# First attention: weighing the values as three bfloat16 products, with the turned rows split by ScalarE and VectorE

## What is computed

```python
def block(args):
    ...
    logits = jnp.einsum('bqhd,bqkd->bqhk', qb.astype(f32), k_sel.astype(f32)) * attn_scale
    logits = jnp.where(valid[:, :, None, :], logits, -jnp.inf)
    p = jax.nn.softmax(logits, axis=-1)
    o = jnp.einsum('bqhk,bqkd->bqhd', p, v_sel.astype(f32))
    return o.astype(qb.dtype)
```

## Time and profile before

| | |
|---|---|
| Time, median of 3 runs | 1764.91 us (1761.79 to 1765.24) |
| The profiled execution: its time | 1763.56 us |
| The profiled execution: its span | 1761.8 us |
| TensorE busy | 1724.0 us (98%) |
| VectorE busy | 1182.8 us (67%) |
| ScalarE busy | 813.6 us (46%) |
| GpSimd busy | 887.1 us (50%) |

### The profile page before, as it was taken

The page is one execution under the profiler, slowest core; times in us unless marked ns, Lnnn a source line. Parts: engine busy times, 40 slices in busy tenths (PEclk is TensorE's granted clock), DMA queues, the critical chain, the costliest instruction groups (busy, mean ns, idle before and its releaser), DMA issues.

```text
span 1761.8 us, 30529 instructions
## 1 busy us (share of the span) xinstructions
PE 1724.0 (98%) x11938; PEld 891.6 (51%) x11938; DVE 1182.8 (67%) x2237; ACT 813.6 (46%) x1628; POOL 887.1 (50%) x805
## 2 busy tenths in 40 slices
PE   8999999999999999999999999999999999999998
PEld 5534455555444466544544455544455555555543
DVE  5759889999999788532345677966155565654637
ACT  4523554443322577412332468733255555555710
POOL 0511443652671222696911177969556555772750
PEclk9999999999999999999999999999999999999999
DMA  9010111102321112212512346512211111111512
GB/s 396 32 54 36 55 49 62 71 37 102 161 96 48 73 67 103 120 48 96 201 63 94 111 145 198 186 54 96 68 40 53 56 42 51 35 52 55 216 58 96
DMA packets 53375, 161.87 MB, mean 92 GB/s; under 512 B 7056, under 2 KB 21776, under 8 KB 49008
## 3 DMA queue, kind: packets, MB, share of 16 engines
q1 hardware_dynamic: 49008, 136.36, 21.8%
q0 software_dynamic: 4224, 23.56, 3.4%
HBM read 129.35 MB, written 27.39 MB: 89 GB/s over the span
## 4 chain that ended last, share of the span: by engine, by line
PE 67%; DVE 20%; ACT 4%; POOL 3%; DMA 3%; issue 2%; SPq 0%; DVEq 0%; ACTq 0%; POOLq 0%
PE ps L1422 28%; PE ps L1901 15%; DVE small L2684 6%; PE ps L1416 4%; DVE arena L2437 4%; PE ps L1762 2%; PE ps L1445 2%; PE ps L1486 2%; PE ps L1544 2%; PE ps L1920 2%; DMA hT<-in_mods 2%; PE ps L1518 1%; PE ps L1694 1%; PE ps L1459 1%; PE ps L1526 1%
## 5 line engine op out<-in xcount | busy, mean ns | idle before, releaser
L1422 PE MATMUL ps<-hT,W 128*128 128x512 bf16 x2424 | 536.5, 380 | 4.1 <-ACT arena L2004 3.2
L1422 PEld LDWEIGHTS ps<-hT,W 128*128 128x128 bf16 x2424 | 235.7, 98 | 288.3 <-issue 10.2
L989 POOL TENSOR_TENSOR W<-W 128x512 bf16<-128x512 f32 x133 | 153.9, 1193 | 248.5 <-DMA W<-in_loads 181.8
L1422 PE MATMUL ps<-W,arena 128*128 128x512 bf16 x936 | 208.2, 380 | 0.0
L2111 ACT ACTIVATE arena<-arena,small 128x128 f32<-128x128 f32 (+9 forms) x192 | 123.1, 642 | 139.0 <-DVE small L2514 119.6
L1422 PEld LDWEIGHTS ps<-W,arena 128*128 128x128 bf16 x936 | 91.2, 97 | 112.0
L2684 DVE TENSOR_SCALAR_CACHE_REDUCE small<-arena,small 128x640 bf16<-128x640 f32 (+1 forms) x124 | 126.5, 1077 | 1.1
L974 POOL TENSOR_TENSOR arena<-arena 128x512 f32<-128x512 f32 (+1 forms) x62 | 104.8, 1690 | 43.9 <-DMA arena<-gates_scratch 20.1
L1422 PE MATMUL ps<-arena,W 128*128 128x512 bf16 x576 | 125.0, 379 | 0.6 <-POOL arena L1050 0.6
L2120 ACT ACTIVATE arena<-arena,small 128x128 f32<-128x128 f32 (+9 forms) x192 | 113.9, 644 | 18.6 <-DVE small L2472 18.6
L1901 PE MATMUL ps<-arena,W 128*128 128x512 bf16 x492 | 112.9, 379 | 0.0
(11 more groups left out here) (392 smaller groups left out, 3223.6 us busy)
## 6 DMA issues: line engine op xcount, KB each, us to landing
W<-in_loads SPq DMA_DIRECT2D x20, 2048.0 KB, 7.9
arena<-sums_scratch SPq DMA_DIRECT2D x30, 512.0 KB, 4.7
W<-in_groups SPq DMA_DIRECT2D x56, 256.0 KB, 3.9
W<-in_loads SPq DMA_DIRECT2D x5, 1792.0 KB, 7.2
gates_scratch<-arena SPq DMA_DIRECT2D x32, 256.0 KB, 2.0
arena<-gates_scratch POOLq DMA_DIRECT2D x2, 4096.0 KB, 13.6
W<-in_mods SPq DMA_DIRECT2D x2, 2048.0 KB, 17.1
hT<-in_mods SPq DMA_DIRECT2D x2, 2048.0 KB, 21.3
```

The costliest lines, as they stand in the source:

```text
L989: last = nc.gpsimd.tensor_tensor(low(v), v, high(v), ALU.subtract)
L1422: last = mm(o, left[:, :, a], moving, start=(k == 0 and (a, b) == PRODUCTS[0]), stop=(k == steps - 1 and (a, b) == PRODUCTS[-1]))
```

## The change

1. The values are split once by GpSimd, behind the weights `ga0`: high and low parts are placed in the unused half of `vw`. The order of the parts counts in `s_parts`, so `FIRST_SPLITS` is 6.
2. `cols` becomes bfloat16 with a low and a high plane, in the same bytes.
3. ScalarE copies each turned group out of PSUM as the high plane (`first_highs`): the first group of item n - 1 between the exponentials and the evacuation of n, the second behind the scaling of n.
4. VectorE makes the low plane by a subtraction that waits for the high plane. Its reciprocal moves ahead of the first group's subtractions.
5. TensorE weighs each key block with three bfloat16 products per half.

```diff
+        v_words = area(10752, 1024).bitcast(BF16).rearrange("p (t c two) -> p t c two", t=NT, two=2)[:, :, 0:DH, :]
+        v_parts1 = area(10752, 1024).bitcast(BF16).rearrange("p (t half two c) -> p t half two c", t=NT, half=2,
+                                                             two=2)[:, :, 1]
...
-        FIRST_SPLITS, PAIR_SPLITS = 5, 4
+        FIRST_SPLITS, PAIR_SPLITS = 6, 4
...
+        def turned_order(i, b0):
+
+            return (1, 0) if i >= FREE_BANK and b0 == 0 else (0, 1)
...
             split("ga0")
+            nc.gpsimd.tensor_copy(v_parts1[:, :, HIGH], v_words[:, :, :, HIGH])
+            nc.gpsimd.tensor_tensor(v_parts1[:, :, LOW], vw[:, :, 0:DH], v_words[:, :, :, HIGH], ALU.subtract)\
+                .then_inc(s_parts, 1)
+            pool.wait_ge(s_parts, 2)
...
                     for j in range(nb):
-                        for x in range(2):
-                            last = mm(ps[halves[x], 1, 0:P], v_of(items[m], x, b0 + j),
-                                      tiles["cols"][g % 2][x][:, j * P:(j + 1) * P], start=(b0 + j == 0), stop=(b0 + j == i))
+                        for vp, cp in PRODUCTS:
+                            for x in range(2):
+                                last = mm(ps[halves[x], 1, 0:P], v_of(b0 + j)[:, vp, :],
+                                          tiles["cols"][g % 2][x][:, cp, j * P:(j + 1) * P],
+                                          start=(b0 + j == 0 and (vp, cp) == PRODUCTS[0]),
+                                          stop=(b0 + j == i and (vp, cp) == PRODUCTS[-1]))
...
+            def first_highs(m, some):
+
+                sems, i = s_att[0], items1[m][2]
+                for g, b0, nb in groups1[m][some]:
+                    for x in turned_order(i, b0):
+                        act.wait_ge(sems["transposed"], 2 * g + x + 1)
+                        if g >= 2:
+                            act.wait_ge(sems["weighted"], g - 1)
+                        A(at1["cols"][g % 2][x][:, HIGH, 0:nb * P], ps[:, turned_bank(i, b0, x), 0:nb * P], ACT.Copy)\
+                            .then_inc(s_high, 1)
...
-                    extra(n, 0)
+                    if tiles is at2:
+                        extra(n, 0)
                     if n >= 1:
-                        high_parts(n - 1)
+                        high_parts(n - 1, slice(0, 1))
+                    if tiles is at1:
+                        extra(n, 0)
                     act.wait_ge(sems["inverse"], n + 1)
...
+                    if n >= 1:
+                        high_parts(n - 1, slice(1, None))
                     extra(n, 1)
...
-                    for x in (1, 0) if i >= FREE_BANK and b0 == 0 else (0, 1):
-                        dve.wait_ge(sems["transposed"], 2 * g + x + 1)
-                        if g >= 2:
-                            dve.wait_ge(sems["weighted"], g - 1)
-                        V.tensor_copy(tiles["cols"][g % 2][x][:, 0:nb * P],
-                                      ps[:, turned_bank(i, b0, x), 0:nb * P]).then_inc(sems["copied"][x], 1)
+                    for q, x in enumerate(turned_order(i, b0)):
+                        dve.wait_ge(s_high, 2 * g + q + 1)
+                        to = tiles["cols"][g % 2][x][:, :, 0:nb * P]
+                        V.tensor_tensor(to[:, LOW], ps[:, turned_bank(i, b0, x), 0:nb * P], to[:, HIGH], ALU.subtract)\
+                            .then_inc(sems["copied"][x], 1)
...
-                    if n >= 1:
-                        copies(n - 1, *groups[n - 1][0])
-                        if n >= 2:
-                            closing(n - 2)
                     if n < len(items):
                         dve.wait_ge(sems["exp"], 2 * n + 2)
                         two = slice((n % 2) * 2, (n % 2) * 2 + 2)
                         V.reciprocal(rden[:, two], den[:, two]).then_inc(sems["inverse"], 1)
                     if n >= 1:
+                        copies(n - 1, *groups[n - 1][0])
+                        if n >= 2:
+                            closing(n - 2)
+                    if n >= 1:
                         for group in groups[n - 1][1:]:
```

More of the change, by code:

```diff
@@ L648, in layer_kernel @@
                                                 "weighted", "read")},
-                 {w: sem(f"att2_{w}") for w in ("scores", "biased", "exp", "inverse", "scaled", "transposed", "high", "copied",
+                 {w: sem(f"att2_{w}") for w in ("scores", "biased", "exp", "inverse", "scaled", "transposed", "copied",
                                                 "weighted", "read")}]
+        s_high = sem("turned_rows_high")
         s_att[0]["copied"] = [sem(f"att1_copied{x}") for x in range(2)]
@@ L743, in layer_kernel @@
         groups1 = groups_of(items1)
+        HIGHS1 = 2 * sum(len(mine) for mine in groups1)
         def products(groups, m):
@@ L2071, in pair_close, with highs @@
                 A(pair_y if j else y2_sum, pair_y, ACT.Square).then_inc(s_ysq, 1)
-            def no_highs(m):
-                return
-            def highs(m):
+            def first_highs(m, some):
[7 more added lines that the diff above has]
+                            .then_inc(s_high, 1)
+            def highs(m, some):
+                if some.start:
+                    return
                 sems = s_att[1]
@@ L2090, in highs, with no_values @@
                         last = A(to[0:far % P, whole:whole + P], ps[0:far % P, 6 + x, whole:whole + P], ACT.Copy)
-                    last.then_inc(sems["high"], 1)
+                    last.then_inc(s_high, 1)
+            def no_values(n):
+                return
             def v_highs(n):
@@ L2120, in pair_attention @@
                         A(t, t, ACT.Copy, scale=rden[:, (n % 2) * 2 + x:(n % 2) * 2 + x + 1]).then_inc(sems["scaled"], 1)
+                    if n >= 1:
+                        high_parts(n - 1, slice(1, None))
                     extra(n, 1)
                     value_parts(n)
-                high_parts(len(items) - 1)
+                for some in (slice(0, 1), slice(1, None)):
+                    high_parts(len(items) - 1, some)
             act.wait_ge(s_par, 16)
@@ L2464, in pair_attention @@
                                                    mneg4[:, (n % 2) * 2 + x:(n % 2) * 2 + x + 1]).then_inc(sems["biased"], 1)
+                    if n < len(items):
+                        dve.wait_ge(sems["exp"], 2 * n + 2)
+                        two = slice((n % 2) * 2, (n % 2) * 2 + 2)
+                        V.reciprocal(rden[:, two], den[:, two]).then_inc(sems["inverse"], 1)
                     if n >= 1:
@@ L2468, in pair_attention @@
                             closing(n - 2)
-                    if n < len(items):
-                        dve.wait_ge(sems["exp"], 2 * n + 2)
-                        two = slice((n % 2) * 2, (n % 2) * 2 + 2)
-                        V.reciprocal(rden[:, two], den[:, two]).then_inc(sems["inverse"], 1)
                     if n >= 1:
@@ L2484, in copies @@
                     for x in range(2):
-                        dve.wait_ge(sems["high"], 2 * g + x + 1)
+                        dve.wait_ge(s_high, HIGHS1 + 2 * g + x + 1)
                         to = at2["cols"][:, m % 2, x]
```

11 lines of the change are left out of this document (6 added, 5 removed).

## The result

The changed kernel takes **1813.78 us** (median of 4 runs, 1809.99 to 1815.34) where the kernel before takes 1764.56 on the same chip (4 runs, 1761.79 to 1765.24): 1.028 times as long, 95% interval 1.0268 to 1.0293. Its profiled execution took 1815.34 us, with a span of 1813.6. The forecast was 1804.3, with a range of 1793 to 1814: the direction was right and so was the place of most of the loss, but the sum was 9.5 us short, and the median lies inside the range by 0.2 us only.

What follows compares the result with a forecast made beforehand. The prediction took TensorE to bound the first attention, and the change to close a ring between VectorE and ScalarE: +40.2 in the attention and +0.5 for GpSimd on 1763.56 us gave 1804.3, range 1793 to 1814.

Steps and rivals of the forecast that it cites:

- The ring: First attention, query blocks i: VectorE waits for ScalarE's high copies before the next biased rows; with i = 0, 1 +40.2; 88%.
- i = 0 and 1: First two query blocks of the attention: TensorE stays the bound, gate-bank evacuations wait behind high copies; +2, bounds 0 and 4.
- ScalarE's copies: First attention: ScalarE makes 96 copies of turned rows, 594 ns at 512 columns; by the totals they would fit.
- The 46 us: Total time of ScalarE's 96 added copies of turned rows in the first attention.
- TensorE's term: Weighing in the first attention: 213 ns per key block becomes 168, 6.5 us less work over 144 blocks, becoming idle from i = 2.
- The 0.17 us bubble: Gap ahead of a full group's weighing at i = 7, subtracted to give 0.85 us, 213 ns per key block.
- the 45 named: Sign that would show the ring: TensorE's idle time grown by about 45 us.
- The clock: First attention, rival: TensorE granted 1.2 GHz from i = 5 on, its doubled work passing the ring; +15, 1819 us; 4%.
- GpSimd's term: Ahead of the attention: two passes splitting the values, 1.65 us, delay the state outputs; +0.5, bounds 0 and 1.65.
- Behind the attention the chain is TensorE's own, so nothing is caught up: Program behind the first attention: the delay carries through without being caught up; no term added.
- slower handovers: Range allowance in the ring: handovers of 0.1 instead of 0.04, with high copies lacking the 0.08 overlap, add 8 us.

Runs made afterwards that it cites:

- products alone: Changed kernel without ScalarE's high copies and without low parts, VectorE in its old order copying each turned row once to bfloat16: 1767.93 us, ratio 1.0027.
- order alone: Kernel before with the reciprocal moved ahead of the copies of turned rows, copies still float32 and made by VectorE: 1775.76 us, ratio 1.0068.
- old order, ScalarE copies: Changed kernel with VectorE's order of before, the first group's low parts ahead of the reciprocal: 1832.23 us, ratio 1.0394.
- both parts by VectorE: Changed kernel with VectorE making high and low parts in the old order, ScalarE making no copies: 1801.86 us, ratio 1.0225.
- rows ahead: Changed kernel with the next item's biased rows made ahead of the second group's low parts, behind items with two groups: 1806.80 us, ratio 1.0250.
- the kernel with the load moved: Changed kernel with one load of weights issued when the decay products are done, not when they begin: 1807.45 us, ratio 1.0248.
- the changed kernel with shifted pieces: Changed kernel with 96 more TensorE products (192 instructions), four per item at i = 2 to 7, overwritten afterwards: 1804.94 us, ratio 1.0234.
- the split alone: Kernel before with only GpSimd's split of the values added, its result read by nobody: 1764.12 us, ratio 1.0005.
- a shift by 64 instructions: Kernel before with 32 more products of 128x16, one ahead of each item's scores, overwritten afterwards: 1770.81 us, ratio 1.0041.

## Why the prediction was right, and where not

| profiled executions, us | before | after | products alone | order alone | old order, ScalarE copies | both parts by VectorE | rows ahead |
|---|---|---|---|---|---|---|---|
| attention | 152.07 | 194.21 | 147.81 | 165.20 | 211.80 | 183.46 | 186.72 |
| VectorE busy in it | 120.2 | 123.7 | 119.1 | 121.2 | 120.2 | 166.2 | 122.9 |
| ScalarE busy in it | 107.6 | 142.2 | 107.5 | 107.8 | 144.5 | 107.8 | 144.2 |

**The ring: right.** The rows were forecast and measured at these lengths, in us. At i = 2: 16.4 and 16.54. At i = 3: 19.6 and 20.36. At i = 4: 23.1 and 23.62. At i = 5: 29.3 and 28.88. At i = 6: 31.7 and 30.92. At i = 7: 39.2 and 39.86. The periods at i = 7 were to be 8.5 and are 8.04 to 8.43, at i = 6 7.6 to 8.2 and are 7.46 to 8.13, at i = 5 7.3 and are 6.94 to 7.32. None of the rows misses by over 0.8 us, and the sum of the attention, +40.2, measured +42.1. (In the kernel with the load moved, whose attention is the same, i = 7 took 40.55, 1.4 over the forecast.) VectorE's idle time per item at i = 7 is 3.18 us (1.31 + 0.31 + 1.56), 3 were named. And it is a ring by experiment: with the same work of ScalarE, VectorE's position moves the attention from 186.7 to 211.8 us.

**i = 0 and 1: near.** +2 forecast, +3.1 measured (13.85 and 20.18 for 13.45 and 17.45). 1.7 of it is clock: the changed kernel with shifted pieces has 18.50 at i = 1, at a mean granted clock of 1.00 where the changed kernel shows 0.92 and 20.18. Without it, +1.4.

**ScalarE's copies: right.** There are 96 of them, 582 ns at 512 columns where 594 were named. The 46 us counted them one by one; ScalarE's busy time in the attention grew by 34.6.

**TensorE's term: right.** 6.5 us of work for 144 blocks is 45 ns per block; 37 to 53 were measured. (The 0.17 us bubble that the reading took off stands ahead of the group, outside the 1.02 us; a like bubble of 0.17 ahead of the next turning's weight loads stands inside.) 24 products stand in the trace as 0.86 us (from 756.88 us, the end modelled). By the 81 ns per product of the Trainium skill, "TensorE: Matmul & The Clock Gate", section "Back-to-back issue gap", they would be an estimated 1.9; the measurement decides against it for this shape. The gain shortened nothing in the changed kernel, as forecast, but it can't be seen there as less work: TensorE's busy time in the attention rose from 144.86 to 153.27 us, at a mean granted clock of 0.93 for 1.00 (the products alone, at 1.00, brought it to 137.13). So its idle time grew by 33.7 us in the attention and by 40.0 in the whole program, not by the 45 named.

**The clock: a rival that came in part, and by the prediction's own signs a miss.** It named a fall of TensorE's clock as a sign of being wrong, and gave 4% to a fall from i = 5 on that would pass the ring, +15. The granted clock did fall, to means of 0.92 to 0.94 in i = 1 and i = 3 to 6 and 0.87 in i = 7, but it never passed the ring. What it costs can be read from rows of other kernels with the same attention that were granted 1.00: 1.7 us at i = 1 (above), 0.8 at i = 3 (19.57 in the kernel with the load moved, 20.36 here) and 1.0 at i = 4 (22.58 and 23.62). So an estimated 3.5 of the 42.1 us are clock, and without them the ring's sum was right or a little high: i = 3 would have been 19.57 for the 19.6 forecast. At i = 5 and 6 no kernel with this attention was granted more, so what the clock costs there isn't shown. Elsewhere it costs ahead of the attention and in the decay products.

**GpSimd's term: right by the median, short in this execution.** It is 0.5 by the median of the kernel that has it alone, within noise, with the idle time grown by 1.6 as the bound had it. It is 2.4 in the profiled execution, because the clock fell behind the longer idle time, as in seven of the nine kernels with the split; the bounds of 0 to 1.65 had left that out.

**"Behind the attention the chain is TensorE's own, so nothing is caught up": the step that failed.** It excluded a gain and, silently, any loss: the term for the rest of the program was 0 and had no upper bound. It measured +8.1 us. No line that the diff names is there, and the load of weights is the same as before; the count of TensorE's instructions is what carried over. Of the 11 us by which the profiled execution exceeds the sum (51.8 for 40.7), 8.1 are this, 1.9 the attention, 1.9 ahead of it, less 0.9 at the end. With that one term, the forecast would have been 1812.4. That the measured median still fell inside the range is luck: the room up to 1814 had been left for slower handovers, the evacuations and GpSimd's split, and what filled it was something else.

What stays open is why 1.2 GHz is granted in just these pieces of the attention. The other stop put down to "issue" (2.6 us at 275 us, 1.0 before) isn't one of instruction pieces: the split alone has it, at 2.63, with TensorE's instructions unchanged. All nine kernels with the split have 2.6 and all three without it 1.0, and the difference is about the 1.65 us of GpSimd's two passes.

## What to carry to other kernels

A step that is split over two in-order engines costs not its instructions but what now waits in front of it on each: write down the ring, item by item, with durations from the rows; here that gave every row from i = 2 on within 0.8 us of the profiled execution. Moving work from a busy engine to an idle one made the kernel slower than doing all of it on the busy one.

A change in the number of an engine's instructions moves the edges of its pieces in all that follows. Look in the timeline for dense runs of short instructions beside a large load, and let the load start behind them.

## What the runs showed of the hardware

- TensorE's instructions come in packets of 16 KB over the DMA engines (97 in 1.59 MB). Where 384 instructions go in 2.9 us while 2 MB of weights are being loaded, it stands still for 3.7 to 5.2 us in six kernels, put down to "issue"; with the load moved behind, 1.1; with the edge moved, 0. In the kernel before the same stretch ran through: its edge lay better, as a shift by 64 instructions shows.
- From the 16 KB packet to TensorE's next product it was 2.3 to 2.5 us in all seven stops.
- The stop costs more than itself: the 48 products of 128x512 behind it took 12.82 us for 10.53, at a mean granted clock of 0.78. Together that is 8.1 us for an idle time of 5.2.
- The same swap of two pieces of VectorE's program was worth +13 us or -18 us of attention, according to which engine made the copies behind it.
- With the same attention code, TensorE was granted 1.00 in one kernel and 0.92 or 0.93 in another in the rows i = 1, 3 and 4; the lower one made these rows 1.7, 0.8 and 1.0 us longer.
